# Moving the sample group's score matmuls behind the second dense group of a tick

## What is computed

```python
def decoder_layer(x, c, attend, conv_prev, ...):
    sh1, sc1, gt1, sh2, sc2, gt2 = ada_mod(c, w_ada, b_ada)            # silu(c) @ w_ada + b_ada
    h = rms_norm(x, rms_g1) * (1 + sc1) + sh1
    q, k, v, hc, bgate, cgate, ga, gb = project_in(h, w_in, q_norm_g, k_norm_g)
    o_att = attend(q, k, v, sb_bias)                                   # stick-breaking attention
    yc, conv_state = short_conv(cgate * hc, conv_prev, conv_w, conv_b) # width 3, causal
    x = x + gt1 * merge_branches(o_att, bgate * yc, ga, gb, w_att_out, w_conv_out, w_o)
    h2 = rms_norm(x, rms_g2) * (1 + sc2) + sh2
    x = x + gt2 * sqrelu_mlp(h2, w_mlp1, w_mlp2)
    return x, k, v, conv_state

def stick_breaking(z, valid):      # A[t,s] = beta[t,s] * prod_{s<j<t} (1 - beta[t,j])
    log_beta = jax.nn.log_sigmoid(z)
    log_keep = jnp.where(valid, jax.nn.log_sigmoid(-z), 0.0)
    suffix = lax.cumsum(log_keep, axis=z.ndim - 1, reverse=True) - log_keep
    return jnp.where(valid, jnp.exp(log_beta + suffix), 0.0)
```

## Time and profile before

| what | value |
|---|---|
| median of 3 runs | 1628.62 us (1628.6 to 1628.83) |
| the profiled execution | 1628.18 us, span 1626.4 us |
| PE busy | 1613.1 us (99%) |
| PEld busy | 1508.1 us (93%) |
| DVE, ACT, POOL busy | 901.0 us (55%), 463.3 us (28%), 607.1 us (37%) |
| granted TensorE clock | 9 of 9 in all 40 slices |
| DMA | 194.76 MB, mean 120 GB/s |

### The profile page before, as it was taken

One profiled execution on the slowest core, in us unless ns is written; L12 is line 12 of the kernel. 1 busy time (PEld: TensorE's weight loads), 2 busy tenths in 40 slices (PEclk: granted clock), 3 DMA queues, 4 the chain that ended last, 5 costly groups with the idle time before them and its releaser, 6 DMA issues.

```text
span 1626.4 us, 31960 instructions
## 1 busy us (share of the span) xinstructions
PE 1613.1 (99%) x12386; PEld 1508.1 (93%) x12386; DVE 901.0 (55%) x1631; ACT 463.3 (28%) x813; POOL 607.1 (37%) x424
## 2 busy tenths in 40 slices
PE   8999999999999999999999999999999999999999
PEld 7998788888888888899999999999999999999999
DVE  5654354554553444325533799556666666666666
ACT  5444222222222222233222452222222222222220
POOL 0245143343344343412121127444444444444440
PEclk9999999999999999999999999999999999999999
DMA  9113446766656676434421111111111111111112
GB/s 382 53 44 99 159 149 216 234 208 235 206 186 222 215 249 230 153 132 174 171 106 40 40 39 53 40 53 53 36 44 53 53 53 53 52 53 53 53 40 107
DMA packets 72230, 194.76 MB, mean 120 GB/s; under 512 B 8049, under 2 KB 8562, under 8 KB 72082
## 3 DMA queue, kind: packets, MB, share of 16 engines
q1 hardware_dynamic: 67682, 178.62, 32.8%
q10 hardware_dynamic: 4400, 14.10, 2.2%
HBM read 174.26 MB, written 18.42 MB: 118 GB/s over the span
## 4 chain that ended last, share of the span: by engine, by line
PE 93%; DVE 2%; DMA 1%; ACT 1%; POOL 1%; issue 1%; SPq 0%; POOLq 0%; DVEq 0%; ACTq 0%
PE psum L827 79%; PE psum L964 2%; PE psum L987 2%; PE psum L1011 2%; PE psum L975 2%; PE psum L1036 2%; PE psum L859 1%; DMA ring<-in_cache_v 1%; POOL wl L728 1%; DVE h2L L1885 1%; DVE sc L1917 1%; DMA xt<-in_xT 0%; PE psum L888 0%; PE psum L995 0%; PE psum L876 0%
## 5 line engine op out<-in xcount | busy, mean ns | idle before, releaser
L810 POOL TENSOR_TENSOR wl<-raw,wh 128x512 fp32r<-128x512 f32 x148 | 212.6, 1441 | 317.2 <-ACT wh L1456 317.0
L827 PE MATMUL psum<-hH,wh 128*128 128x352 f32 x808 | 268.9, 333 | 0.1
L827 PE MATMUL psum<-hL,wh 128*128 128x352 f32 x808 | 260.0, 322 | 0.0
L827 PE MATMUL psum<-hH,wl 128*128 128x352 f32 x808 | 259.3, 321 | 0.0
L827 PE MATMUL psum<-hidH,wh 128*128 128x352 f32 x768 | 247.4, 322 | 0.0
L827 PE MATMUL psum<-hidH,wl 128*128 128x352 f32 x768 | 247.2, 322 | 0.0
L827 PE MATMUL psum<-hidL,wh 128*128 128x352 f32 x768 | 247.1, 322 | 0.0
L753 POOL TENSOR_TENSOR beta<-beta,kb 128x512 f32<-128x512 f32 (+3 forms) x96 | 122.5, 1296 | 248.7 <-DVE kb L1677 248.7
L728 POOL TENSOR_TENSOR wl<-raw,wh 128x1024 fp32r<-128x1024 f32 x49 | 119.6, 2440 | 231.4 <-ACT wh L1318 230.9
L827 PEld LDWEIGHTS psum<-hH,wh 128*128 128x128 f32 x808 | 151.5, 188 | 30.4 <-issue 29.3
L2004 DVE SCALAR_TENSOR_TENSOR act<-psum,mods,act 128x352 f32<-128x352 f32 x256 | 145.4, 580 | 50.5 <-PE psum L827 50.5
(11 more groups left out here) (255 smaller groups left out, 3254.9 us busy)
## 6 DMA issues: line engine op xcount, KB each, us to landing
raw<-in_weights SPq DMA_DIRECT2D x152, 512.0 KB, 3.7
ring<-in_cache_k SPq DMA_DIRECT2D x128, 256.0 KB, 3.9
ring<-in_cache_v SPq DMA_DIRECT2D x128, 256.0 KB, 3.7
pre<-in_weights SPq DMA_DIRECT2D x16, 512.0 KB, 16.6
gate_scratch<-gt ACTq DMA_DIRECT2D x14, 528.0 KB, 3.5
act<-gate_scratch SPq DMA_DIRECT2D x14, 528.0 KB, 4.6
xt<-in_xT SPq DMA_DIRECT2D x8, 528.0 KB, 6.9
act<-in_xT SPq DMA_DIRECT2D x8, 528.0 KB, 4.7
```

Of the source, the lines that this page charges most:

```text
L810: pool.tensor_tensor(xl, source_of(i), x.bitcast(F32), ALU.subtract).then_inc(S["split"], 1)
L827: mm = pe.matmul(out, x, y, start=n == 0, stop=n == end)
```

## The change

In every tick with two dense groups, the second one is written ahead of the sample's scores. The same is done in `SLOTS`, which sorts SP's loads.

```diff
-SLOTS = ("scores", "dense_a", "sturn", "turn", "sscore", "dense_b", "ada", "sav", "av")
+SLOTS = ("scores", "dense_a", "sturn", "turn", "dense_b", "sscore", "ada", "sav", "av")
...
                     ada_turn(ADA_TURN_AT[k], ada_ps)
+                if k in DENSE_B and k:
+                    dense(DENSE_B[k], hH, hL)
                 if k in ITEM_AT:
                     sample_scores(ITEM_AT[k], k)
-                if k in DENSE_B and k:
-                    dense(DENSE_B[k], hH, hL)
                 if k in ADA_AT:
```

## The result

The change makes the kernel slower: 1656.56 us median (1654.77 to 1658.13, 4 runs) against 1628.72 us (1628.6 to 1628.87, 4 runs), a ratio of 1.017 (95% interval 1.0158 to 1.0182). The forecast was 1650 us, with a range of 1641 to 1661.

The account below looks back on a forecast made before the run. PE, busy 541.68 of the mix stage's 545 us, was taken as the bound. Seven new waits, 23.8 us, less 2.5 us saved, added 21.3 us to 1628.18: 1649.5, rounded to 1650 us, range 1641 to 1661.

Parts of the forecast that it names:

- The places: PE waits newly in ticks 5, 9, 13, 21, 29, 33 and 37, 23.8 us in all; likeliest case, chance 0.65.
- The chain through ACT, POOL and SP: Ticks 8, 12, 32, 36: weight splitting behind `sbeta` moves the values' load by 3.9 us; next ticks wait 2.8 to 3.7 us.
- the queue's order in two ticks: Ticks 4 and 28: values' load now stands behind a weight load on SP; ticks 5 and 29 wait 3.6 and 4.1 us.
- the convolution: Tick 20, DVE: it stands between the sample's scan and `ada_copy`, so tick 21's scores wait 3.2 us (2.5 to 3.9).
- a lower bound: Tick 9: wait of 3.7 us for values, at least 2.9, held up by the convolution's DVE chain, which also moves 3.9 us.
- some 20: Sign in the changed trace: PE L1036 waits for values' loads six times, some 20 us, against two times and 0.9 before.
- The line of tick 13: Values' load issued at 331.86 + 3.9, plus 6.0 for transfer, lands at 341.8 against use at 338.71: wait of 3.1 us.
- The saving: On PE, fewer switches save 0.25 us per double tick (0.12 to 0.3); ten of 17 keep it, 2.5 us.
- a risk for other ticks: Rival of more waits: chains held covered are not, such as `ada_copy` in ticks 4, 32, 36; 1655 to 1662 us, chance 0.1.
- The clock: Rival: clock falls to 1.2 GHz behind each of seven waits, up to 4 us each, 28 us more, 1678 us; chance 0.1.
- stretches at a lower clock: Sign against the prediction: granted clock should stay 1.00; low-clock stretches after the waits would show it wrong.
- other waits: Upper range, to 1661 us, took in most further waits from uncovered chains or delayed ring loads, 5 to 10 us; chance 0.1.

Follow-up runs that it names:

- the run with ACT's order: Changed kernel, but on ACT the high half of the weights goes ahead of the sample's probability in all ticks: 1646.93 us, ratio 1.0103.
- the run with SP's: Changed kernel with only SP's order of loads put back as before, PE's new order kept: 1650.89 us, ratio 1.0135.
- tick 20 alone: Kernel before, with the swap made only in tick 20: 1633.54 us, ratio 1.003.
- both cures: Changed kernel with SP's loads in the order of before and ACT's high half ahead of the sample's probability in ticks 8, 12, 32 and 36: 1631.63 us.
- fitted fillers: Changed kernel with 10 to 14 useless matmuls in front of each of the seven waits, the number fitted to each: 1648.79 us, ratio 1.0122.
- 9 fillers: Changed kernel with 9 useless matmuls in front of each of the seven waits: 1650.06 us, ratio 1.0124.
- the kernel with twelve ticks: Kernel before with the swap only in twelve double ticks, and ACT's high half ahead of the sample's probability in ticks 12, 32 and 36: 1625.17 us.

## Why the prediction was right, and what it missed

**The places.** All seven, and none besides. The values' loads were issued where the forecast had them: within 0.1 us in ticks 5 and 29, and in tick 32, measured against the tick's start, 3.9 us later. The chain through ACT, POOL and SP is shown by the run with ACT's order in ticks 13, 33 and 37, the queue's order in two ticks by the run with SP's, the convolution by tick 20 alone. With both cures 2.5 us are left. In tick 9 both chains were late: DVE's took 2.70 us of the wait, where the forecast had used it only as a lower bound, and the transfer ended last by 0.97 us. So the waits of L1036 came to 15.7 us, not the "some 20" that the forecast named as a sign.

**The size of the waits.** The last column of the table has them for the changed kernel: ticks 5, 9, 13, 21, 29, 33 and 37 were late by 3.27, 4.06, 3.18, 3.41, 3.45, 2.01 and 2.77 us, 22.2 us in all, and the forecast had 3.6, 3.7, 3.1, 3.2, 4.1, 3.3 and 2.8, 23.8 us. Tick by tick it is off by up to 1.3 us, because the landing of four DMAs scatters: tick 33's took 5.2 us where 7.0 were taken. In the kernel with fitted fillers the same sum is 25.2 us, so that the forecast lies between the two is in part luck. Two of its workings are loose. The line of tick 13 adds 6.0 us for the transfer where the paragraph above it says 6.4 (it took 5.75), and the waits of ticks 5 and 29 and the bounds of ticks 5, 29, 33 and 37 come out 0.1 to 0.2 us lower when they are added up from their terms.

**The saving.** I priced it at 0.25 us in the ten ticks. It was 0.23 to 0.33 us, in all 17, some 4.5 us; in the seven others it is part of my 3.9 us instead of 4.0, so I had counted a little of it there. Tick 19, behind the swap of tick 18, lost 0.2 us: `ada_copy` stands behind the later scan there and had no slack, which the forecast had named as a risk for other ticks.

**The clock.** This is the step that failed. The forecast left it out of the sum and kept it as a rival, with a chance of 0.1, at up to twice a dense group's 4.01 us in each place, and named stretches at a lower clock behind the waits as a sign that it would be wrong. That sign came. The clock fell in all seven places of the profiled execution and cost 12 us there, 1.4 to 2.8 us in each, not 4: it belonged into the likeliest case, at a smaller price. The argument against it ("the waits of before, up to 0.65 us, did nothing") said nothing on waits of 3 us, as I noted myself. The price was too high since the clock was back soon: in tick 5 the two rows just behind the wait were slow, L1036 with 1.94 us and `values` with 1.60, and the scores that followed took 1.13 us, as in the run with fillers.

**The range** held the time because its upper side was kept for other waits, not for this. That is luck: the sum of 1628.2 + 22.2 - 4.5 gives 1646 us for the changed kernel at full clock (an estimate from its own ticks), 4 us under the forecast, and the 12 us of the clock bring it to the 1658 us of the profiled execution. Waits priced too high and a saving priced too low had hidden part of what the clock added.

Open: why the clock held at two waits of 2.5 and 3.0 us. And why the landing of a set of four DMAs takes 5.2 us in one kernel and 7.1 in another for the same item. The traffic of the gates' spills and of a weight load just ahead in the queue is the suspect; it was not tried separately.

## What to carry to other kernels

Where one engine is busy 99% of the time, moving a small step behind a large one cost nothing on that engine here, and all of the loss came from what hung on the small step. So follow each semaphore that it raises through the in-order queues of the other engines, up to the DMA queue, and compare the shift with the slack between landing and use. A wait of 2 us or more can cost more than its own length, since TensorE often came back from it at half speed here, for 1.4 to 2.8 us more in each place. And a reordering that loses as a whole can win in the ticks where nothing hangs on it: pick them from the trace.

## What the runs showed of the hardware

The granted clock fell for waits of PE that are short against a tick: at 19 of 21 places with 2.0 us of idleness or more it went to 0.5 for a stretch, in the two others (3.04 us with SP's order of before, 2.47 us with 9 fillers) and in all with up to 1.44 us it stayed at 1.00. Each fall cost 1.4 to 2.8 us beyond the wait in the changed kernel, 12 us for seven. Matmuls of no use in the wait, 0.233 us each for 128x128 in float32, kept the clock up in all executions with 20 or a fitted number of them, and brought the median down by 7.8 us. Going from small tiled matmuls (L1011) to `ada` (L859) instead of to a dense group, and entering them from a dense group, saved 0.23 to 0.33 us together. The last landing of the four DMAs of 256 KB that ticks 5, 9, 13, 29, 33 and 37 wait for came, over all kernels here, between 5.0 us (tick 5, before) and 8.7 us (tick 33, the kernel with twelve ticks) after the first one's issue.
